# Scan of a delta-rule mixer: first products of the inverse merged, sum Z as one 128-row product, the state kept twice

## The reference, cut to what matters

```python
def rwkv7_scan(r, w, k, v, a_vec, b_vec):
    def step(S, inp):
        r_t, w_t, k_t, v_t, a_t, b_t = inp
        sa = jnp.einsum('bhvk,bhk->bhv', S, a_t)
        S = S * w_t[:, :, None, :] + sa[..., None] * b_t[:, :, None, :] + v_t[..., None] * k_t[:, :, None, :]
        y = jnp.einsum('bhvk,bhk->bhv', S, r_t)
        return S, y
    S0 = jnp.zeros((B, H, N, N), jnp.float32)
    _, y = lax.scan(step, S0, xs)
```

## Time and profile before

| | us |
|---|---|
| median of 3 runs | 3730.86 |
| lowest, highest | 3730.16, 3739.53 |
| span of the profiled execution | 3730.1 |
| scan, first to last matmul | 1599.6 to 1945.4 |
| PE busy, whole run | 3484.1 |
| DVE busy, whole run | 2548.5 |
| ACT busy, whole run | 1510.4 |

### The profile page before, as it was taken

One profiled execution on the slowest core, in us unless ns is written; L12 is line 12 of the kernel. 1 busy time (PEld: TensorE's weight loads), 2 busy tenths in 40 slices (PEclk: granted clock), 3 DMA queues, 4 the chain that ended last, 5 costly groups with the idle time before them and its releaser, 6 DMA issues. The chain is left out here.

```text
span 3730.1 us, 55202 instructions
## 1 busy us (share of the span) xinstructions
PE 3484.1 (93%) x23684; PEld 2843.4 (76%) x23684; DVE 2548.5 (68%) x2261; ACT 1510.4 (40%) x1620; POOL 1188.1 (32%) x544
## 2 busy tenths in 40 slices
PE   8999999999999998977788999999998999997996
PEld 6778788887877776667776788887877888886875
DVE  5563767678767875966657667678867888857532
ACT  4563533334443336844446432334454122125322
POOL 1225445445532211243433444555531000000211
PEclk9999999999999999978999999999999999998998
DMA  2112123354312243842323133344312222234422
GB/s 101 39 52 65 55 95 110 102 180 140 115 55 99 79 144 111 261 145 83 105 65 125 48 102 107 103 169 151 106 60 95 84 79 74 79 124 100 146 94 107
DMA packets 218755, 387.50 MB, mean 104 GB/s; under 512 B 16321, under 2 KB 118849, under 8 KB 214529
## 3 DMA queue, kind: packets, MB, share of 16 engines
q1 hardware_dynamic: 180944, 311.62, 26.1%
q10 hardware_dynamic: 37568, 72.36, 5.2%
HBM read 277.50 MB, written 105.91 MB: 103 GB/s over the span
## 5 line engine op out<-in xcount | busy, mean ns | idle before, releaser
L3912 POOL MEMSET ssm_toep<- 128x4096 f32 x1 | 3.5, 3512 | 538.9 <-POOLq L3578 538.9
L3439 DVE SCALAR_TENSOR_TENSOR H<-hy_cu,par,H 128x1024 f32<-128x1024 f32 x120 | 153.5, 1279 | 0.0
L270 POOL TENSOR_TENSOR wlo1C<-fast_raw,whi1C 128x1024 fp32r<-128x1024 f32 (+1 forms) x40 | 112.5, 2813 | 112.7 <-ACT whi1C L260 112.7
L270 POOL TENSOR_TENSOR wlo0B<-fast_raw,whi0B 128x1024 fp32r<-128x1024 f32 (+1 forms) x40 | 113.0, 2825 | 106.0 <-ACT whi0B L260 106.0
L270 POOL TENSOR_TENSOR wlo1A<-fast_raw,whi1A 128x1024 fp32r<-128x1024 f32 (+1 forms) x40 | 111.5, 2787 | 104.0 <-ACT whi1A L260 104.0
L270 POOL TENSOR_TENSOR wlo0A<-fast_raw,whi0A 128x1024 fp32r<-128x1024 f32 (+1 forms) x40 | 110.7, 2768 | 103.5 <-ACT whi0A L260 103.5
L270 POOL TENSOR_TENSOR wlo1B<-fast_raw,whi1B 128x1024 fp32r<-128x1024 f32 (+1 forms) x39 | 107.7, 2762 | 112.1 <-ACT whi1B L260 111.9
L3439 DVE SCALAR_TENSOR_TENSOR hy_odd<-hy_cu,par,hy_odd 128x1024 f32<-128x1024 f32 x112 | 143.3, 1279 | 0.0
L1008 DVE TENSOR_TENSOR fast_xl<-fast_xr,fast_xh 128x2048 fp32r<-128x2048 f32 (+1 forms) x42 | 127.7, 3062 | 21.4 <-ACT fast_xh L849 21.4
L270 POOL TENSOR_TENSOR wlo0C<-fast_raw,whi0C 128x1024 fp32r<-128x1024 f32 (+1 forms) x39 | 108.0, 2768 | 104.1 <-ACT whi0C L260 104.0
L2717 PE MATMUL psA<-sc_XX,sc_NT 64*64 64x32 f32 x2560 | 104.8, 232 | 31.8 <-issue 18.8
(11 more groups left out here) (1459 smaller groups left out, 11601.9 us busy)
## 6 DMA issues: line engine op xcount, KB each, us to landing
fast_raw<-ffn_in_dram SPq DMA_DIRECT2D x88, 512.0 KB, 3.9
fast_xr<-ffn_x SPq DMA_DIRECT2D x28, 1024.0 KB, 6.2
fast_raw<-ffn_out_dram SPq DMA_DIRECT2D x32, 512.0 KB, 3.8
sc_ops<-rw_arbkv SPq DMA_DIRECT2D x14, 1024.0 KB, 6.0
wraw1A<-hybrid_in_dram SPq DMA_DIRECT2D x24, 512.0 KB, 3.5
wraw1B<-hybrid_in_dram SPq DMA_DIRECT2D x24, 512.0 KB, 3.5
ffn_x<-fast_g ACTq DMA_DIRECT2D x22, 512.0 KB, 3.2
ffn_x<-fast_e ACTq DMA_DIRECT2D x22, 512.0 KB, 2.8
```

Source lines behind the costliest of these rows:

```text
L270: eng.tensor_tensor(self.slot(wlo, n), self.raw[n], self.slot(whi, n).bitcast(fp32), ALU.subtract)\
L3439: op = dve.scalar_tensor_tensor(out=acc, in0=c[:, j:j + T], scalar=w, in1=acc, op0=ALU.mult, op1=ALU.add)
L3912: pl.memset(toep[:, :, :], 0.0).then_inc(*tick("st_zero"))
```

## The change: what it does

- W of a level is made by eight matmuls instead of sixteen, in one burst ahead of X's sixteen, no longer alternating with them. To this end the transpose of X is kept apart (`XT`, three buffers) in a block form: for head half e only the crossed half of the partitions is filled and the rest is zero, cleared once by DVE. One matmul takes all 128 rows of NT against the columns of both heads. The result for pair m lands in `half(m%2)` of the bank, so that a copy to `Wt` takes four ACT instructions of 64x128 instead of one of 128x256, and X waits for all four.
- Z is one product of 128 rows for each head: G's free half of the first 64 columns receives A (by DMA from memory, after the raw scores have been copied away), and UV's free half receives the state. The separate buffer of A goes. A's load is four DMAs for a pair of chunks instead of one.
- The state is held in swapped halves, written by DVE once as S and once more into UV (two products of 64x512 ahead of that of S). `pc` and R are stored in swapped halves, with two ACT copies for one and two DMAs for one.
- The ring of NT has five buffers instead of six, and constants have other addresses.

```diff
+                self.XX = at("sc_XX", [P, 4, DT, CHUNK], fp32, 113.25)
+                self.XT = at("sc_XT", [P, 3, 2, DT, CHUNK], fp32, 121.25)
+                self.NT = at("sc_NT", [P, 5, DT, CHUNK], fp32, 133.25)
-                self.at = at("sc_at", [P, DT, 2 * CHUNK], fp32, 172.25)
...
-                        act.activation(pc[:, m, :], pex[:, z, :, CHUNK], ACT.Copy).then_inc(*tick("op_pc"))
+                        for e in range(2):
+                            act.activation(pc[(1 - e) * HEAD:(2 - e) * HEAD, m, :], pex[e * HEAD:(e + 1) * HEAD, z, :, CHUNK], ACT.Copy)\
+                               .then_inc(*tick("op_pc"))
...
+            paired = [b.rearrange("p (e g t) -> p e g t", e=2, g=4) for b in bank]
+            def part_of_two(t, l):
+                return t.rearrange("p e (g b c) -> p e g b c", b=2, c=2 << l)[:, :, :, 0, :]
...
-                    def load_a(p):
-                        if p >= 1:
-                            sp.wait_ge(*after("pe_Z", 2 * p))
-                        sp.dma_start(at[:, :, :], QD[p, :, :, AT, :]).then_inc(*tick("at_in", 16))
+                    def load_a(n):
+                        sp.wait_ge(*after("sc_raw", 4 * n + 4))
+                        for e in range(2):
+                            sp.dma_start(G[half(1 - e), n % 4, e, :, 0:CHUNK], QD[n // 2, half(e), :, AT, (n % 2) * CHUNK:(n % 2 + 1) * CHUNK])\
+                              .then_inc(*tick(f"at_in_{n % 4}", 16))
...
+                        load_a(2 * p)
+                        load_a(2 * p + 1)
                         if p >= 1:
-                            load_a(p)
                             load_r(p)
...
+                    def grow(w):
+                        cw, lw = w
+                        iw = order[w]
+                        if lw == 0:
+                            pe.wait_ge(*after("sc_turned", 2 * cw + 2))
+                        else:
+                            pe.wait_ge(*after("sc_XT", 2 * turned_order[cw, lw - 1] + 2))
+                        pe.wait_ge(*after("sc_NT", iw + 1))
+                        for m in range(DT):
+                            mw = pe.matmul(part_of_two(paired[iw % 2][half(m % 2), :, m // 2, :], lw), NT[:, iw % NTS, m, :],
+                                           part_of_two(XT[:, cw % TURNS, :, m, :], lw), start=True, stop=True)
+                        mw.then_inc(*tick("pe_W"))
+                    def spread(x):
+                        cx, lx = x
+                        ix = order[x]
+                        pe.wait_ge(*after("sc_W", 4 * ix + 4))
+                        if ix >= 2:
+                            pe.wait_ge(*after("sc_XX", ix - 1))
+                        for m in range(DT):
+                            for e in range(2):
+                                mx = pe.matmul(part_of_tile(eight[2 + ix % 2][half(e), m, :], lx, 1), Wt[lx][half(e), m, :],
+                                               part_of_tile(XX[half(e), cx % 4, m, :], lx, 1), start=True, stop=True)
+                        mx.then_inc(*tick("pe_XX"))
                     def inverse(w, x):
+                        if w is not None:
+                            grow(w)
                         if x is not None:
+                            spread(x)
...
                     def zed(n):
-                        pe.wait_ge(*after("at_in", 16 * (n // 2 + 1)))
-                        pe.wait_ge(*after("sc_S", n + 1))
+                        pe.wait_ge(*after(f"at_in_{n % 4}", 32 * (n // 4 + 1)))
+                        pe.wait_ge(*after("sc_SU", 2 * n + 2))
                         enter(pe, ("Z", n))
                         for m in range(DT):
                             for e in range(2):
-                                pe.matmul(eight[place(("Z", n))][half(e), m, :], G[half(e), n % 4, e, m, 0:CHUNK], UV[half(e), n % 4, e, m, :],
-                                          start=True, stop=False)
-                            for e in range(2):
-                                mm = pe.matmul(eight[place(("Z", n))][half(e), m, :], at[half(e), m, a * CHUNK:(a + 1) * CHUNK], S[half(e), a, m, :],
-                                               start=False, stop=True)
+                                mm = pe.matmul(eight[place(("Z", n))][half(e), m, :], G[:, n % 4, e, m, 0:CHUNK], UV[:, n % 4, e, m, :],
+                                               start=True, stop=True)
...
-                        act.activation(part(Wt[l][:, :, :], l, 0), part(eight[i % 2], l, 0), ACT.Copy).then_inc(*tick("sc_W"))
+                        for q in range(2):
+                            for e in range(2):
+                                act.activation(part_of_two(Wt[l][half(e), q:DT:2, :], l), part_of_two(paired[i % 2][half(q), e, :, :], l),
+                                               ACT.Copy).then_inc(*tick("sc_W"))
...
                         dve.wait_ge(*gone(("S", n)))
+                        if n >= 3:
+                            dve.wait_ge(*after("pe_y", n - 2))
+                        for e in range(2):
+                            dve.tensor_tensor(UV[half(1 - e), (n + 1) % 4, e, :, :], grown[half(1 - e), :, :],
+                                              pc[half(1 - e), :, n:n + 1].to_broadcast([HEAD, DT, HEAD]), ALU.mult).then_inc(*tick("sc_SU"))
...
+                    for e in range(2):
+                        dve.memset(UV[half(1 - e), 0, e, :, :], 0.0).then_inc(*tick("sc_SU"))
+                    dve.memset(XT[:, :, :, :, :], 0.0).then_inc(*tick("sc_clear"))
+                    dve.wait_ge(*after("sc_clear", 1))
```

More of the change, by code:

```diff
@@ L2714, in inverse @@
-                        for m in range(DT):
-                            if w is not None:
-                                for e in range(2):
-                                    mw = pe.matmul(part_of_tile(eight[iw % 2][half(e), m, :], lw, 0), NT[half(1 - e), iw % NTS, m, :],
-                                                   part_of_tile(XX[half(1 - e), cw % 4, 1, m, :], lw, 0), start=True, stop=True)
-                                if m == DT - 1:
-                                    mw.then_inc(*tick("pe_W"))
-                            if x is not None:
-                                for e in range(2):
-                                    mx = pe.matmul(part_of_tile(eight[2 + ix % 2][half(e), m, :], lx, 1), Wt[lx][half(e), m, :],
-                                                   part_of_tile(XX[half(e), cx % 4, 0, m, :], lx, 1), start=True, stop=True)
-                                if m == DT - 1:
-                                    mx.then_inc(*tick("pe_XX"))
+                            spread(x)
@@ L2759, in state @@
                             for e in range(2):
-                                mm = pe.matmul(eight[place(("S", n))][half(e), m, :], BK[:, n % 4, e, m, :], UV[:, n % 4, e, m, :],
+                                mm = pe.matmul(eight[place(("S", n))][half(1 - e), m, :], BK[:, n % 4, e, m, :], UV[:, n % 4, e, m, :],
                                                start=True, stop=True)
@@ L2824, in to_xx @@
                         for e in range(2):
-                            act.activation(XX[half(e), n % 4, 0, :, :], G[half(1 - e), n % 4, e, :, 0:CHUNK], ACT.Copy).then_inc(*tick("sc_raw"))
+                            act.activation(XX[half(e), n % 4, :, :], G[half(1 - e), n % 4, e, :, 0:CHUNK], ACT.Copy).then_inc(*tick("sc_raw"))
                     def to_gx(n):
```

62 lines of the change are left out of this document (26 added, 36 removed).

## The result

The changed kernel takes 3715.85 us (median of four runs, 3714.25 to 3717.76); the kernel before, in the same comparison, 3734.82. The ratio is 0.9948, 95% interval 0.9933 to 0.9963: 14 to 25 us faster. The forecast was 3716.5, and the measured time lies inside the range of 3686 to 3746. In the profiled executions the span went from 3730.1 to 3714.4, -15.7.

What follows compares the result with a forecast made beforehand. PE was taken to be bound by its instruction supply. Twelve scan periods at -17, the last two 0, start +2.2 and small copies +0.3 gave -14.5, so 3716.5 us on the median; range 3686 to 3746.

Steps and rivals of the forecast that it cites:

- Supply of instructions: In the scan, PE runs out of instructions at packet ends: 4.9 packets of 4.28 us make a 20.9 us period.
- PE's own work: PE's matmul streams in a scan period grow from 13.8 to 15.9 us, +2.1, with a slot at 1.5 us.
- Packets: PE's instructions a period fall from about 1,245 to 1,020, 4.0 packets; idle at their edges falls to some 1.5 us.
- 0.7 us a period: Allowance on the scan loop's 18.4 us for stalls and low clock not hidden in it, giving 19.1 us.
- The loop: PE, DVE and ACT wait in turn in the scan: even periods 19.8 us, odd 17.0, mean 18.4 without stalls.
- the chain of the prediction: Odd periods: scores out at 11.1, copies to XX, Z, W, then PE's X, U and K's transposes: 17.0 us.
- The last two periods: Scan's latency-bound end: shorter W and Z cancel longer ACT and DVE steps, 0, between -3 and +3 us.
- The start: DVE's clearing of XT and UV halves delays the first score eviction from 1601.69 to 1604.1: +2.2 us, 4 at most.
- Rival 1: Instruction supply alone sets the scan period, 17.1 to 18 us, the loop having more slack: 3683 to 3698 us; chance 0.20.
- Rival 2: The scan's loop eats the gain, as stalls and chains lengthen each other: 20.2 us a period, 3729 us; chance 0.22.
- rival 4: Merging doesn't lower the instruction count, each wide matmul being split again: slower than 3746 us; 2%, counted within 0.16.
- rival 3: PE's longer scan work keeps the old packet-edge stalls: 21.6 us a period, 3746 us; chance 0.16 including the split-matmul case.

Runs made afterwards that it cites:

- e1_burst: Kernel before, with all sixteen W matmuls of a slot run first and then all sixteen of X, instead of alternating; ratio 0.9998.
- e3_z_only: Kernel before with only the Z part: one 128-row product per head, state written twice in swapped halves, A loaded into G, W and X as before; ratio 0.9953.
- e4_b_first: Changed kernel, with ACT copying the last two of turned B ahead of the last W in even periods; ratio 0.9921 to the kernel before.
- e11_half_w_copy: Changed kernel, with ACT copying W of only half of the head pairs out of PSUM; ratio 0.9914 to the kernel before.
- e6_w_best: Kernel before with only the merged W, plus B's last copies before the last W copy and XT cleared behind the first score eviction; ratio 0.9921.
- e8_all: Changed kernel with three edits: state products on POOL, B's last copies before the last W copy, XT cleared late; ratio 0.9924 to the kernel before.
- W alone: Kernel before with only the merged W, its XT, four ACT copies and rings; Z, state and load of A as before; ratio 0.9926.

## Why the prediction was right

**What bounds the kernel before.** Supply of instructions: right, by e1_burst (some 4 us more of PE work a period at no cost in time, 2.2 of them out of idle time at packet edges) and, more weakly, by e3_z_only, whose period follows its packets at nearly the same pace (4.22 against 4.31).

**PE's own work.** Right in size. The timeline of PE in the changed kernel:

```profile
1721.66 0.67 PE L2720 MATMUL psA<-sc_XT,sc_NT 128*64 128x64 f32 x16
1722.25 1.06 PE L2733 MATMUL psB<-sc_XX,sc_Wt 64*64 64x32 f32 x30
1723.11 0.33 PE L2693 MATMUL psC<-sc_ops 64*64 64x128 f32 x2
```

W has 16 records and X starts 0.59 us after it (0.48 and a pass of 0.1 were forecast); the scores start at 1723.11, so that the slot takes 1.45 (1.5 forecast). A period has some 980 records (11,714 in twelve); by the program there are 1,020, as forecast, and the rest are missing from the trace.

**Packets.** 47 in the stretch, 3.9 a period; 4.0 forecast. The idle time left at their edges was put at 1.5 us a period and is 0.2 (2.4 us in all). That figure of the mechanism was clearly off; the likely reason is that with 4.8 us of time for a packet even those delayed by data come in time. Of the 0.7 us a period that were added to the loop for it and for the low clock, its part wasn't needed.

The Trainium skill, Runtime: NRT & Kernel Launch, section Instruction fetch mechanics, has the fetch hidden; here it is so in the changed kernel (2.4 us), and not in the kernel before (58 us).

**The other engines.** A W copy of 64x128 takes 273 ns (296 forecast), two state products 1.40 us (1.36 forecast), ACT is busy 13.1 us a period (13.7), DVE 14.8 (15.0).

```profile
L2832 ACT ACTIVATE sc_Wt<-psA 64x128 f32<-64x128 f32 x320 | 87.3, 273 | 47.7 <-PE psA L2720 41.0
...
1722.32 1.40 DVE L3001 TENSOR_TENSOR sc_UV<-sc_grown,rw_pc 64x512 f32<-64x512 f32 x2
```

**The loop.** Its even form came as worked out. From the first W at 1717.4 the scores are out at 1728.7, 11.3 us (11.1 forecast); ACT's chain takes 7.9 (7.9); V's transposes wait 2.5 us, and the period is 19.3 to 20.9 (19.8). That the wait and ACT's copies are on the path of the even periods is shown by e4_b_first and e11_half_w_copy. "DVE then has no break" holds too: from the first X on to the scores DVE waits for nobody in ten of the twelve periods, and for 0.2 and 0.4 us in the other two. What the loop leaves out is that PE stands right beside DVE there. Take the 1.4 us of products away, and PE's X comes last: 0.8 us of them are gained in an even period, and none in an odd one that starts at the low clock.

Odd periods take 17.3 to 17.6 (17.0 forecast), but not by the chain of the prediction, which runs from the scores over ACT's copies, Z and W to PE's X, U and K. What ends last before the next S is this:

```profile
1714.36 1.27 POOL L2922 TENSOR_TENSOR sc_XX<-sc_XX,sc_eye 128x512 f32<-128x512 f32 x1
...
1715.67 1.44 DVE L2965 STREAM_TRANSPOSE sc_XT<-sc_XX 64x512 f32<-64x512 f32 x2 [1.79 <-POOL sc_XX L2922]
...
1718.98 0.65 DVE L2990 COPY sc_UV<-psD 64x512 f32<-64x512 f32 x1
...
1719.77 1.15 PE L2771 MATMUL psD<-sc_UV,sc_BK 128*64 128x64 f32 x32 [0.63 <-DVE sc_UV L2990]
```

The copied scores go through two products of POOL (2.6 us from 1713.01), DVE waits 1.79 us for them, then works without a break up to its copy of U, and S on PE waits 0.63 us for that (0.5 or 0.6 us at the end of each of the six odd periods). The forecast chain is done 0.8 us earlier (0.20 us of a wait for NT and these 0.63). So the 17.0 was near by luck, the two chains being nearly as long; and it fits that e11_half_w_copy, with its shorter W copies, left the odd periods alone.

The mean is 18.8 against 18.4 without stalls and 19.1 with the allowance.

**The low clock.** It was one of the reasons for the 0.7 us allowed, and it comes after the new wait, though not each time. Windows of PE's wait and of what follows, twice:

```profile
1697.50:1700.20 2.70, 0.18 (x8) 0.08 (x4) 2.51 (x5) 2.53 (x8) 2.70 (x4) 1.00 0.06 14
1700.20:1704.00 3.80, 3.80 (x114) 3.62 (x116) 1.31 (x3) 2.77 (x7) 2.46 (x2) 1.00 0.36 100
1734.00:1736.70 2.70, 0.22 (x8) 0.08 (x4) 2.56 (x5) 2.53 (x8) 2.70 (x4) 0.98 0.00 1
1736.70:1741.00 4.30, 4.27 (x70) 4.00 (x72) 0.20 (x1) 2.44 (x7) 2.50 (x3) 0.50 0.35 91
```

After the same 2.5 us of waiting PE went on at 2.4 GHz once (114 records in 3.8 us) and at 1.2 GHz once (70 in 4.3). The three even periods with such a drop last 20.9, the others 19.3 to 19.7: 1.4 us each, 4 us in all.

**Last periods, start, small edits.** The last two periods were put at 0 and gave 3.8; e3_z_only, with Z alone, gave 1.5 of it there. The start was put at +2.2 (its own figures, 1604.1 and 1601.69, give 2.4). The first score eviction starts 3.3 us later than in the earlier trace rows:

```profile
1602.34 2.62 DVE L3009 MEMSET sc_XT<- 128x3072 f32 x1 [0.59 <-issue]
1604.99 1.29 DVE L2959 TENSOR_TENSOR sc_G<-psC,sc_mask 128x512 f32<-128x512 f32 x2
```

It costs that much at its place, and 2.9 at the first W; the rest of the 5.8 was for the most part the granted clock of this run, as the comparison with e4_b_first shows. A's loads put 34.1% on the data queue instead of 26.0% and "issue" is 2.4 us in all: the 0 that was taken for them fits, though nothing tested it by itself.

**In sum.** Forecast -17 + 0 + 2.2 + 0.3 = -14.5; in the traces -20.0 - 3.8 + 5.8 + 2.3 = -15.7. Middle and end gave 7 us more than forecast, start and tail took 6 more. The total is as close as it is because these errors cancel. There is luck in the 3716.5 as well: it was counted from a median of 3730.86, and beside the changed kernel the kernel before had 3734.82, so that the fall of the medians is 19.0 us where 14.3 were forecast. The mechanism is right for the kernel before and for the even periods; for the odd ones the length came out, and the chain didn't.

**Rivals.** Rival 1 (supply alone, 17.1 to 18 a period) isn't the changed kernel, which waits for ACT at 18.8; e6_w_best with 18.0 comes near it, but its PE is busy nearly all the time. Rival 2 (20.2 a period) and rival 4 (no fewer instructions) are refuted by the windows, rival 3 by e1_burst.

**What stays open.** The kernels e4, e6 and e8 all end at 0.992, though their stretches run from 211 to 223 us in the profiled runs; four or five runs of each do not tell them apart, and one profile is one draw of the clock. Also open: what bounds e6_w_best, why the Z part costs something on top of the merged W, and why the granted clock fell after some waits and not after others.

Three orders are faster than the kernel before and very likely than the changed one: e4_b_first (0.9921), e6_w_best (0.9921) and e8_all (0.9924). Their intervals end at 0.9934 to 0.9936, and that of the changed kernel, timed in another comparison, begins at 0.9933. e6_w_best does it without the Z part, and W alone (0.9926) nearly as well.

## What to carry to other kernels

When an engine idles for "issue", divide its records by its instruction packets and cut windows at the idle times: if all hold the same number of records, then instructions are the currency, and larger matmuls can win even where they lose arithmetic. Then price the loop that is next before merging more: here a product whose result needs four small copies instead of one moved the bound of every second period to the engine that copies, and the order there was worth some 10 us. Before an engine's work is taken out of a loop, look for who stands right beside it: of DVE's 1.4 us only 0.8 were to be had. And split a mean by kind of period, for the odd and the even ones had different limits. Two gains that are both paid out of the same stall don't add.

## What the runs showed of the hardware

- A packet of some 252 instructions of PE was not had faster than 4.22 us on the mean of twelve periods in any kernel here. In the three with the most "issue" it was 4.22 to 4.31, with PE busy 186 to 215 us of the stretch (the kernel before, e1_burst, e3_z_only); one packet more or less changes these by 2%.
- Waits that are already met are not free: 26 of them ahead of a slot cost about 0.5 us in the changed kernel, a part of it "issue", and they take only about half as many instructions of the fetched stream as they are in number (five packets for 2,470 waits).
- The same scan work, once at a granted clock of 0.73 and once at 1.00 over 19 us, made the first S come some 5 us apart in two kernels that differ by one order on ACT (after, e4_b_first).
- POOL takes 1308 ns for the 64x512 product that DVE makes in 686, and the time stayed the same (0.9955 against 0.9948).

```profile
L2942 POOL TENSOR_TENSOR sc_UV<-sc_grown,rw_pc 64x512 f32<-64x512 f32 x30 | 39.2, 1308 | 48.3 <-DVE sc_grown L3011 47.1
```
